# A two-block transformer kernel: the normalization's scale behind the products in three more places, the memory loaded in quarters, and six attention heads moved to later rounds

## The reference

```python
h = rmsnorm(x, g[0]); y = hybrid_mixer(h, ...)          # 12 dilated attention heads, gating, 12 recurrent heads
x = x + rmsnorm(y, g[1])
h = rmsnorm(x, g[2])
y = memory_cross_attention(h, rmsnorm(mem, mem_src_gain), wq, wkv, wo)   # 4 heads of 128, 256 memory tokens
x = x + rmsnorm(y, g[3])
h = rmsnorm(x, g[4])
y = conv_ffn(h, w_up, conv_w, conv_b, w_down)           # up to 2 x 5632, 3 taps, gelu gate, down
x = x + rmsnorm(y, g[5])

def rmsnorm(x, gain):
    return x * rsqrt(mean(x * x, axis=-1) + eps) * gain
```

## Time and profile before

| | |
|---|---|
| median of three runs | 2446.37 us (2443.76 to 2446.81) |
| profiled execution | 2443.64 us, span 2441.9 us |
| TensorE busy | 2288.3 us, 94% |
| VectorE, ScalarE, GpSimd busy | 1346.7, 1060.7, 52.0 us |
| mean granted clock of TensorE | 0.965 of full |
| DMA | 373 MB, mean 153 GB/s |

### The profile page before, as it was taken

How to read it: one execution, slowest core, us unless ns; L and a number is a source line. 1 busy time by engine, 2 the same in 40 slices (tenths; PEclk the granted TensorE clock), 3 DMA queues, 4 the chain that set the end, 5 groups by cost and what they waited for, 6 DMA issues and landing times.

```text
span 2441.9 us, 31690 instructions
## 1 busy us (share of the span) xinstructions
PE 2288.3 (94%) x13034; PEld 1984.1 (81%) x13034; DVE 1346.7 (55%) x1681; ACT 1060.7 (43%) x1358; POOL 52.0 (2%) x61
## 2 busy tenths in 40 slices
PE   7999997969987999999999999999998999999898
PEld 6888976858875888888888888788976789898676
DVE  5545655375555566666657444744455555444654
ACT  4433441223454545545546333533444443343543
POOL 0000010011000000000000000000000000000000
PEclk9999987979988999999999999999999999999899
DMA  8556520000643455555565555565530556555033
GB/s 284 163 177 215 183 76 1 1 31 30 230 155 104 147 185 186 188 189 189 189 200 192 194 190 191 167 219 162 192 121 1 172 173 229 168 192 166 1 121 138
DMA packets 235158, 373.03 MB, mean 153 GB/s; under 512 B 8311, under 2 KB 108196, under 8 KB 234020
## 3 DMA queue, kind: packets, MB, share of 16 engines
q1 hardware_dynamic: 228272, 360.41, 44.9%
q10 hardware_dynamic: 6772, 10.98, 1.3%
HBM read 369.25 MB, written 2.12 MB: 152 GB/s over the span
## 4 chain that ended last, share of the span: by engine, by line
PE 63%; DVE 6%; issue 5%; ACT 2%; DMA 0%; POOL 0%; DVEq 0%; POOLq 0%; ACTq 0%; SPq 0%
PE PS L449 16%; PE PS L412 12%; PE PS L414 11%; PE PS L413 11%; PE PS L452 8%; PE PS L1850 2%; DVE w_lo L335 1%; PE PS L1834 1%; DVE small L1887 1%; ACT w_hi L330 1%; DVE spare L1883 1%; PE PS L856 0%; PE PS L2475 0%; ACT spare L1862 0%; DVE h_both L873 0%
## 5 line engine op out<-in xcount | busy, mean ns | idle before, releaser
L335 DVE TENSOR_TENSOR w_lo<-raw,w_hi 128x2048 fp32r<-128x2048 f32 (+2 forms) x340 | 766.6, 2255 | 798.7 <-ACT w_hi L330 798.6
L330 ACT ACTIVATE w_hi<-raw 128x2048 fp32r<-128x2048 f32 (+2 forms) x340 | 641.2, 1886 | 850.4 <-PE PS L414 489.8
L449 PE MATMUL PS<-h_both,w_hi 128*128 128x512 f32 x1968 | 539.1, 395 | 2.2 <-DVE h_both L873 1.4
L412 PE MATMUL PS<-w_hi,h_both 128*128 128x512 f32 (+2 forms) x1344 | 512.1, 381 | 18.2 <-DVE h_both L878 12.0
L413 PE MATMUL PS<-w_lo,h_both 128*128 128x512 f32 (+2 forms) x1344 | 509.1, 379 | 0.0
L414 PE MATMUL PS<-w_hi,h_both 128*128 128x512 f32 (+2 forms) x1088 | 409.8, 377 | 0.0
L449 PEld LDWEIGHTS PS<-h_both,w_hi 128*128 128x128 f32 x1968 | 336.7, 189 | 48.9 <-DVE h_both L873 2.7
L452 PEld LDWEIGHTS PS<-h_both,w_lo 128*128 128x128 f32 x1968 | 301.9, 189 | 42.0
L452 PE MATMUL PS<-h_both,w_lo 128*128 128x256 f32 x1968 | 313.0, 281 | 0.0
L412 PEld LDWEIGHTS PS<-w_hi,h_both 128*128 128x128 f32 x1344 | 255.6, 190 | 66.8 <-DVE h_both L878 12.7
L413 PEld LDWEIGHTS PS<-w_lo,h_both 128*128 128x128 f32 x1344 | 255.5, 190 | 46.4
(11 more groups left out here) (503 smaller groups left out, 2028.5 us busy)
## 6 DMA issues: line engine op xcount, KB each, us to landing
raw<-in_w_in SPq DMA_DIRECT2D x132, 1024.0 KB, 5.2
raw<-in_ffn_w_up SPq DMA_DIRECT2D x176, 512.0 KB, 4.4
raw<-in_w_out SPq DMA_DIRECT2D x48, 1024.0 KB, 5.1
raw<-in_ffn_w_down SPq DMA_DIRECT2D x44, 1024.0 KB, 5.1
raw<-in_mem_wkv SPq DMA_DIRECT2D x8, 1024.0 KB, 7.2
raw<-in_mem_wq SPq DMA_DIRECT2D x4, 1024.0 KB, 5.5
raw<-in_mem_wo SPq DMA_DIRECT2D x4, 1024.0 KB, 5.1
raw<-in_w_in SPq DMA_DIRECT2D x4, 768.0 KB, 4.6
```

Of the source, the lines that this page charges most:

```text
L330: act.activation(w_hi[:, slot % 2, :st.n], raw[:, slot, :st.n], ACT.Copy).then_inc(hi_made, 1)
L335: dve.tensor_tensor(w_lo[:, slot % 2, :st.n], raw[:, slot, :st.n], w_hi[:, slot % 2, :st.n].bitcast(F32), ALU.subtract).then_inc(lo_made, 1)
L412: pe.matmul(ps, l_hi, r_hi, start=start, stop=False, skip_group_check=skip)
L449: pe.matmul(sums, wh[:, k, cs], h_both[:, :, kk, :], start=kk == 0, stop=False, skip_group_check=True)
```

## The change

Four edits, all in the order and form of existing steps:

1. The memory's k and v: `mem` is loaded in four quarters of its columns on two queues, ident first; the transposes read the unscaled rows; the scale multiplies k (as a row) and v (as a column) when they leave PSUM. The bias product moves from the start to between k's and v's products. The trip of its result through memory (`scratch`, `hankel`) moves behind v. `x` is loaded behind the small constants. ScalarE loads its table with a tiny activation.
2. The memory's q: unscaled opening; its scale goes into the softmax (the exponential's scale and the negated maximum).
3. The up product: unscaled opening; each group's evacuation gets one more product on VectorE, with the scale's row. The first two groups stand outside TensorE's loop.
4. The mixer: each side lane has a pause of nine rounds behind its first three heads.

```diff
-        to_channels(ST_MEM_K, K_MEM, 0)
-        to_tokens(ST_MEM_V, v_mem, 0)
...
+        class Pause:
+
+            kind, rounds = "pause", 9
+
+        HEADS_FIRST = 6
+        LANE_JOBS = [side_jobs[0:HEADS_FIRST:2] + [Pause] + side_jobs[HEADS_FIRST::2] + [finishes[0], finishes[2]],
+                     side_jobs[1:HEADS_FIRST:2] + [Pause] + side_jobs[HEADS_FIRST + 1::2] + [a_norm, finishes[1]]]
...
+                               scale=mem_pos[:, t_:t_ + 1] if job["name"] == "mem" else job["scale"],
+                               accum_out=den[:, t_:t_ + 1]).then_inc(j.act, 1)
...
+                if job["name"] == "mem":
+                    dve.wait_ge(n_memq.dve, n_memq["neg"])
+                    dve.tensor_tensor(nm, nm, mem_neg, ALU.mult).then_inc(j.dve, 1)
+                else:
+                    dve.tensor_scalar(nm, nm, -job["scale"], None, ALU.mult).then_inc(j.dve, 1)
...
+        def mem_scale_vector(dve):
+            dve.wait_ge(n_memq.act, n_memq["sq"])
+            mean_vector(dve, n_memq, n_memq.ssq.rearrange("p (t g) -> p t g", t=TB))
+            dve.wait_ge(n_memq.pool, n_memq["rstd"])
+            dve.tensor_scalar(mem_pos, n_memq.rstd, M_D ** -0.5, None, ALU.mult).then_inc(n_memq.dve, 1)
+            dve.tensor_scalar(mem_neg, n_memq.rstd, -(M_D ** -0.5), None, ALU.mult).then_inc(n_memq.dve, 1)
...
+        up_scale = []
+
         def up_vector(dve, q):
+            scale, = up_scale
             dve.wait_ge(act_evac, q.number(1))
             up = rows_up[:, q.parity, :, :]
-            dve.tensor_tensor(up, up, wide_sums(q, 1), ALU.add).then_inc(dve_evac, 1)
+            dve.tensor_tensor(up, up, wide_sums(q, 1), ALU.add).then_inc(added, 1)
+            dve.wait_ge(scale.dve, scale["row"])
+            dve.wait_ge(added, q.plus(2, q.c + 1))
+            dve.tensor_tensor(up, up, scale.row.unsqueeze(1).to_broadcast([P, 4, S]), ALU.mult).then_inc(dve_evac, 1)
...
+            group(Group(ST_UP, 1), row)
+            group(Group(ST_UP, 2))
+            with pe.Fori(0, UP_TURNS - 1) as i:
+                group(Group(ST_UP, 3, i))
+                group(Group(ST_UP, 4, i))
...
+            next(scale)
+            run(group_vector(dve, Group(ST_UP, 1), before=Group(ST_UP, 0), between=scale))
...
-        n_mem, t_mem = norm_job(), turn_job()
+        n_mem, t_mem = scale_job(None, MEM_ROW, MEM_TILE, "sq1 mean", Chain(new, "mem_norm")), turn_job()
+        scaled_to_channels(ST_MEM_K, K_MEM, 0, n_mem)
+        scaled_to_tokens(ST_MEM_V, v_mem, 0, n_mem)
+        mem_rows = ar(0, TB, D)
+        mem_squared = new("mem_squared")
...
-        add_out = add_job()
-        n_memq, t_memq = added_norm_job(add_out), turn_job()
+        add_out = quarters_add_job()
+        n_memq, t_memq = scale_job(add_out, dve="sum mean pos neg"), turn_job()
         t_o = turn_job(M_H, single=False)
-        add_mem = add_job()
-        n_ffn, t_ffn = added_norm_job(add_mem), turn_job()
+        add_mem = quarters_add_job()
+        n_ffn, t_ffn = scale_job(add_mem, FF_ROW, FF_TILE), turn_job()
+        up_scale.append(n_ffn)
...
+        def mem_scale_steps(dve):
+            j = n_mem
+            dve.scalar_tensor_tensor(out=cat[:, 1, :], in0=mem_rows[:, 1, :], scalar=1.0, in1=mem_rows[:, 1, :],
+                                     op0=ALU.mult, op1=ALU.mult, accum_out=j.ssq[:, 1:2]).then_inc(j.dve, 1)
+            dve.wait_ge(mem_squared, 1)
+            dve.wait_ge(j.dve, j["sq1"])
+            dve.tensor_scalar(j.rstd, j.ssq[:, 0:2], 1.0 / D, EPS, ALU.mult, ALU.add).then_inc(j.dve, 1)
+            yield
+            steps = scale_row_vector(dve, j, MEM_BANK)
+            next(steps)
+            yield
+            next(steps)
+            dve.wait_ge(bias_job.pe, bias_job["rows"])
+            dve.tensor_copy(arena[0:A_H, WROW:WROW + 384], PS[0:A_H, 7, 0:384]).then_inc(bias_job.dve, 1)
...
+            pe.wait_ge(ident_in, 16)
+            run(products_tensor(pe, ST_MEM_K, opening_tensor(pe, ST_MEM_K, t_mem, blocks_of(mem_rows), mem_ready)))
+            scale_row_tensor(pe, n_mem, MEM_BANK)
             pe.wait_ge(bias_job.dve, bias_job["one"])
             pe.wait_ge(rel_in, 32)
             pe.matmul(PS[0:A_H, 7, 0:384], arena[0:REL + 1, TBL:TBL + A_H], arena[0:REL + 1, ONEHOT:ONEHOT + 384],
                       start=True, stop=True).then_inc(bias_job.pe, 1)
...
+            pe.wait_ge(n_mem.dve, n_mem["row"])
+            pe.wait_ge(bias_job.dve, bias_job["copied"])
+            pe.wait_ge(exch_in, 16)
...
+            run(products_tensor(pe, ST_MEM_Q, opening_tensor(pe, ST_MEM_Q, t_memq, blocks_of(x), quarters_ready(add_out))))
...
+            up_tensor(pe, opening_tensor(pe, ST_UP, t_ffn, blocks_of(x), quarters_ready(add_mem)), n_ffn)
...
+            mem_cols = I["mem"][0].rearrange("(t p) d -> p t d", p=P)
+            act.dma_start(ident[:, :], I["ident"]).then_inc(ident_in, 16)
+            act.dma_start(mem_rows[:, :, quarter(0)], mem_cols[:, :, quarter(0)]).then_inc(mem_in[0], 16)
+            act.dma_start(params[:, :], I["params"]).then_inc(params_in, 16)
+            act.dma_start(mem_rows[:, :, quarter(1)], mem_cols[:, :, quarter(1)]).then_inc(mem_in[1], 16)
+            act.wait_ge(bias_job.dve, bias_job["half"])
+            act.activation(table_first, minus_half, ACT.Square)
+            act.wait_ge(params_in, 16)
             run(products_scalar(act, ST_MEM_K, more=True,
-                                opening=opening_scalar(act, ST_MEM_K, t_mem, gain_of("g_src"), rows)))
-            act.wait_ge(rel_out, 16)
-            act.dma_start(hankel, bass.AP(I["scratch"].tensor, 0, [[1, P], [384, A_H], [1, S]])).then_inc(rel_back, 16)
+                                opening=unscaled_opening_scalar(act, ST_MEM_K, t_mem, gain_of("g_src"), made=0)))
+            act.activation(cat[:, 0, :], mem_rows[:, 0, :], ACT.Square, accum_out=n_mem.ssq[:, 0:1]).then_inc(mem_squared, 1)
...
+            act.wait_ge(bias_job.dve, bias_job["copied"])
+            act.dma_start(I["scratch"], arena[0:A_H, WROW:WROW + 384]).then_inc(rel_out, 16)
...
+            mean_vector(dve, add_out, ssq4[0])
+            dve.wait_ge(add_out.pool, add_out["rstd"])
+            quarters = quarters_vector(dve, add_out)
+            some(quarters, 2)
+            run(products_vector(dve, ST_MEM_Q, more=True,
+                                opening=unscaled_opening_vector(dve, ST_MEM_Q, t_memq, gain_of("g_mem"), quarters)))
+            mem_scale_vector(dve)
+            last_vector(dve, end_of(ST_MEM_Q))
...
-            sp.wait_ge(mem_in, 16)
-            products_sync(sp, ST_MEM_K)
+            mem_cols = I["mem"][0].rearrange("(t p) d -> p t d", p=P)
+            load_units(sp, Group(ST_MEM_K, 0), 0, 1)
+            for c in (2, 3):
+                sp.dma_start(mem_rows[:, :, quarter(c)], mem_cols[:, :, quarter(c)]).then_inc(mem_in[c], 16)
+            load_units(sp, Group(ST_MEM_K, 0), 1, 4)
+            sp.dma_start(exch[:, :], I["exch"]).then_inc(exch_in, 16)
+            sp.dma_start(arena[0:REL, TBL:TBL + A_H], I["rel_bias_table"]).then_inc(rel_in, 16)
+            sp.dma_start(arena[0:REL + 1, ONEHOT:ONEHOT + 384], I["onehot"]).then_inc(rel_in, 16)
...
-            sp.wait_ge(add_out.dve, add_out["x11"])
+            sp.wait_ge(add_out.dve, add_out["x3"])
```

More of the change, by code:

```diff
@@ L1757, in late_gpsimd, with rounds @@
             run(together(*[finish_gpsimd(pool, e.j, e.j, e.j.lane["var"], e.vb) for e in LATE]))
+        def rounds(n):
+            for _ in range(n):
+                yield
         def side_tensor(pe, j):
-            if j.kind == "head":
+            if j.kind == "pause":
+                yield from rounds(j.rounds)
+            elif j.kind == "head":
                 yield from dilated_tensor(pe, j)
@@ L2008, in up_scalar_program, with up_vector_program @@
             run(group_scalar(act, end_of(ST_UP), before=Group(ST_UP, ST_UP.groups - 2)))
-        def up_vector_program(dve, opening):
+        def up_vector_program(dve, opening, scale):
             run(opening)
-            run(group_vector(dve, Group(ST_UP, 1), before=Group(ST_UP, 0)))
+            next(scale)
+            run(group_vector(dve, Group(ST_UP, 1), before=Group(ST_UP, 0), between=scale))
             run(group_vector(dve, Group(ST_UP, 2), before=Group(ST_UP, 1)))
@@ L2805, in _ @@
             run(products_scalar(act, ST_OUT, opening=out_opening_scalar(act), ahead=ST_MEM_Q))
-            rows = changed_scalar(act, n_memq, x, cat)
-            some(rows, 4)
-            run(products_scalar(act, ST_MEM_Q, opening=opening_scalar(act, ST_MEM_Q, t_memq, gain_of("g_mem"), rows)))
+            run(products_scalar(act, ST_MEM_Q, opening=unscaled_opening_scalar(act, ST_MEM_Q, t_memq, gain_of("g_mem"),
+                                                                               squares_scalar(act, n_memq))))
             on_all_lanes(act, lane_scalar, mem_lanes)
@@ L2896, in _ @@
             dve.wait_ge(gained, 4)
```

(6 more changed lines are left out.)

85 lines of the change are left out of this document (32 added, 53 removed).

## The result

The changed kernel takes 2428.57 us (median of 4 runs, 2427.42 to 2429.46) against 2445.07 for the kernel before beside it: ratio 0.9936, 95% interval 0.9924 to 0.9949, 16.5 us less. A second set of five runs gave 0.9940 (0.9926 to 0.9953). The forecast was 2421 in a range of 2410 to 2432, with 23.3 us of gain. The profiled execution took 2427.42, its span 2425.6.

The account below looks back on a forecast made before the run. TensorE was taken as the bound, busy 94% of the span, so only its gaps and half clock could yield time. Start -7.3, memory's q -6.6, up product -6.1 and mixer -3.3 gave -23.3: 2421 us, range 2410 to 2432.

Parts of the forecast that it names:

- The likeliest case: Whole kernel: the summed gain of 23.3 us comes true, giving 2421 us; chance 0.55.
- start bound by loads: Rival at the start: first product at 16 us or a wait for x, total 2423 to 2426; chance 0.08.
- The high end of the range, -12: Whole kernel: the smallest gain, with all terms at their high ends, given as -12 us.
- Start: Loads and opening up to k's and v's products: first product at 12.9 us; -7.3 us (-8.5 to -4.1).
- if SyncE's queue moves as much meanwhile: Early loads: both queues move equal bytes, 1.68 MB in all, so params land at 6.8 us.
- the upper bound: Start: all SyncE issues ahead (2.1 MB) goes first, params at 10.0, first product at 16.1 us, saving 6.0.
- Memory's q: Opening of the memory's q: unscaled transposes start sooner, 8.03 us becoming 1.47; -6.6 us.
- Up product: Its opening and 22 groups: 6.56 idle and 0.7 clock gained, 0.8 and 0.4 of costs; -6.1 us.
- Mixer: Recurrence rounds with later heads 3 to 5, norm and finishes: summed to -3.3 us (-11.2 to +3.4).
- the twins: Mixer: each stretch takes as long as an earlier-trace stretch with the same contents, such as 16.02 for rounds 15 to 19.
- the term of the finishes: Mixer rounds 39 to 47: attention norm and three finishes moved there add 7 us, from 3.2 up to 9.7.
- Extra step on VectorE: Rival in the up product: VectorE's added product, above 3.6 us, costs 22 times the excess; slower than before, chance 0.05.

Follow-up runs that it names:

- Experiment 6: Changed kernel with its first loads in order of need, plus ten TensorE transposes of ident ahead of the wait for quarter 1: 2427.47 us.
- Experiment 4: Changed kernel with three more 128x1024 products on VectorE, results thrown away, in each of the up product's 22 groups: 2473.17 us.
- experiment 7: Changed kernel with eight dilated heads ahead of a pause of four rounds, instead of six heads and nine rounds: 2432.72 us, ratio 0.9952.
- the loads in order: Changed kernel, SyncE's queue bringing quarter 0 then four weight units, ScalarE's ident, params, quarters 1 to 3: 2426.99 us, ratio 0.9936.

## Why the prediction was right, and where it was off

The range, 22 us wide, held the time. The likeliest case was off by 7 to 8 us: a part of that is the rival "start bound by loads" (2423 to 2426), which came true as such, and the second block put 5 on top. The high end of the range, -12, is -13.4 by its own terms (-4.1 - 6.6 - 6.1 + 3.4).

- **Start**, forecast -7.3, measured -3.3. The step that failed is "if SyncE's queue moves as much meanwhile". SyncE's queue went first (0.78 MB to 0.00 from 3 to 5 us), and the product came at 16.09. That this is the 16.1 of the upper bound is luck. The bound let all 2.1 MB of SyncE's early items go first, which puts the params at 10.0; in the run only the first item, 1.05 MB, did. ScalarE's queue had moved 0.83 of its 0.86 MB at 9 us, and the params were in use at 10.25, about an us behind their last bytes, which no term had. The chain behind them took 5.8 for 6.1. The Trainium skill ("DMA: Bandwidth & Descriptors", Queues, rings and completion order) has the engines go round the queues that have work: the trace agrees from 5.4 us on (0.40 to 0.39 MB from 7 to 9) and not ahead of it, unless ScalarE's queue had nothing ready by then, which no run shows. The measured -3.3 lies outside the term's own bounds, -8.5 to -4.1. In the sum: 6.05 us for the first product; 1.4 lost at the half clock behind it, which no term had and which is why the bounds failed; 1.1 for the row and the bias product between k and v (1.9 forecast); 0.2 is left over.
- **Memory's q**, -6.6 and -7.0: right; the idle time is 4.76 (4.85 at the up product), inside the 4.7 to 5.3 given.
- **Up product**, -6.1 and -5.9: right in sum. The idle time gave 6.56, and the rest of the stage took 0.7 more, for 0.5 forecast (0.8 and 0.4 of costs less 0.7 of clock). The gap for the row was 0.33. The clock gave less than its 0.7: 0.92 behind the opening, up from 0.82, and not the 1.00 taken from layer 2, and layer 2 itself has 0.78 there this time, so the 1.00 of one row was chance. The Trainium skill ("TensorE: Matmul & The Clock Gate", Part 4: PE-mode transpose) says that transposes don't count as work for the clock. Experiment 6 contradicts it: there TensorE went to the full pace behind 18 to 22 transposes and nothing else.
- **Mixer**, -3.3 and -5.4 (-4.5 by the runs of that part alone): the twins held to 0.1 us where the clock is full, and the second opening was 62.3 to 64.1 in the nine profiles with this order, for 61.6. Mis-sized was the term of the finishes, 7 for 5.3, and 1.0 came from the first opening, whose work did not change.
- **Extra step on VectorE**: below its threshold, as argued. Experiment 4 finds the wait that the two slacks give (1.53 for 1.55) and a second one behind it. In all it costs 2.0 us a group for 3.8 us added, so the threshold of 3.6 us may be too high by some tenths.
- **Not in the sum at all**: the second block, +5.4. The terms of the touched stages add up to within 1.5 us of the forecast, and the total still fell short, because code that nobody touched spent more time at the half clock.

## What to carry over

Work out a start by the item with the longest chain behind it, not by the bytes of both queues, and put nothing first on an early queue that the first product doesn't need. Sum by twins from the same trace wherever the clock is full; where it is not, the same code varies by 2 us a stretch, so a gain of a few us needs several profiles of either kernel before a stage is blamed for what is missing. And an order that moves work out of one stage still pays for it in the next: count what the moved work costs there (experiment 7: 9.1 us for the norm and the finishes, 5.3 where they stood).

## What the runs showed of the hardware

- Of two queues that had been issued to from 0.8 us on, SyncE's had the DMA engines alone from 3 to 5 us (0.78 MB to 0.00) in the changed kernel, and each had half (0.40 and 0.39 MB from 7 to 9) once SyncE's first item, 1.05 MB, was through. With a first item of 0.52 MB on SyncE's queue, ScalarE's moved 0.12 MB from 3 to 5 us.
- fp32 transposes alone took TensorE from 1.2 to 2.4 GHz (eight took 1.97 us, later ones 1.36), and behind 3.7 us of idle time it was back at 1.2 (granted clock 0.50 at 15.2 us).
- The column of the granted clock read 1.00 at 16 to 20 us of the changed kernel, where the matmuls ran at half pace (9 and 11 in 2 us, 18 and more from 20 us on): at the start of a trace the pace is the better witness.
- Executions of one kernel differ by up to 6 us (2423.19 to 2429.00 with the loads in order, 2422.38 to 2428.52 in experiment 6). Between profiles, such differences stand where TensorE has gaps and the granted clock differs: the same stretch took 133.1 us at 0.94 and 135.5 at 0.92.
